# Decays of a blocked linear recurrence: from products with 0/1 matrices to one running sum and its differences

## What is computed

```python
b = jnp.cumsum(gc, axis=1)                       # running sum of the logs in a chunk
o_inter = jnp.einsum('bchk,bhkv->bchv', qc * jnp.exp(b), S)
diff = b[:, :, None] - b[:, None, :]
decay = jnp.exp(jnp.where(tril[None, :, :, None, None], diff, -jnp.inf))
scores = jnp.sum(qc[:, :, None] * kc[:, None] * decay, axis=-1)
o_intra = jnp.einsum('bijh,bjhv->bihv', scores, vc)
S = jnp.exp(b_last)[..., None] * S + jnp.einsum('bjhk,bjhv->bhkv', kc * jnp.exp(b_last[:, None] - b), vc)
```

## Time and profile before

| what | value |
|---|---|
| runs | 3353.06, 3353.88, 3355.38 us |
| median | 3353.88 us |
| profiled execution, first to last instruction | 3349.8 us |
| median less this span | 4.1 us |
| PE busy | 3183.6 us (95%) |
| DVE busy | 1477.6 us (44%) |
| ACT busy | 994.6 us (30%) |
| POOL busy | 638.9 us (19%) |
| mean granted TensorE clock | 0.984 |

### The profile page before, as it was taken

The page is one execution under the profiler, slowest core; times in us unless marked ns, Lnnn a source line. Parts: engine busy times, 40 slices in busy tenths (PEclk is TensorE's granted clock), DMA queues, the critical chain, the costliest instruction groups (busy, mean ns, idle before and its releaser), DMA issues. The chain is left out here.

```text
span 3349.8 us, 50802 instructions
## 1 busy us (share of the span) xinstructions
PE 3183.6 (95%) x19854; PEld 2885.0 (86%) x19854; DVE 1477.6 (44%) x2589; ACT 994.6 (30%) x2077; POOL 638.9 (19%) x951
## 2 busy tenths in 40 slices
PE   6999988988999999999989998898999999999999
PEld 5997666657999999999989966666589999999998
DVE  5312556655443344333372035665545443333443
ACT  4222345444321121211142233553433212111111
POOL 2113656521200000000031145663211000000000
PEclk8999999999999999999999999999999999999999
DMA  6415811103111111111123262111210111111101
GB/s 215 138 68 163 260 41 60 37 17 130 38 51 38 38 42 59 50 38 38 38 79 106 95 197 87 54 52 29 97 64 26 38 63 50 38 38 38 50 25 54
DMA packets 192340, 237.17 MB, mean 71 GB/s; under 512 B 18697, under 2 KB 166494, under 8 KB 192190
## 3 DMA queue, kind: packets, MB, share of 16 engines
q1 hardware_dynamic: 137276, 158.44, 14.7%
q10 hardware_dynamic: 44354, 45.25, 4.3%
q0 software_dynamic: 10560, 31.44, 2.6%
HBM read 195.53 MB, written 39.56 MB: 70 GB/s over the span
## 5 line engine op out<-in xcount | busy, mean ns | idle before, releaser
L1550 PE MATMUL banks<-act_split,w_split 128*128 128x384 f32 (+1 forms) x8352 | 1390.0, 327 | 11.1 <-DVE act_split L2294 11.1
L1550 PEld LDWEIGHTS banks<-act_split,w_split 128*128 128x128 f32 x8352 | 1378.4, 188 | 17.9 <-DVE act_split L2294 10.1
L1550 PE MATMUL banks<-hidden_split,w_split 128*128 128x384 f32 (+1 forms) x3168 | 528.3, 327 | 0.0
L1550 PEld LDWEIGHTS banks<-hidden_split,w_split 128*128 128x128 f32 x3168 | 524.7, 188 | 0.9 <-issue 0.6
L2352 DVE SCALAR_TENSOR_TENSOR x<-banks,mod,x 128x384 f32<-128x384 f32 (+2 forms) x768 | 353.6, 496 | 193.3 <-PE banks L1550 190.8
L2801 DVE TENSOR_TENSOR hidden_f<-banks,silu_a 128x384 f32<-128x384 f32 x132 | 70.7, 535 | 736.4 <-PE banks L1550 736.4
L1550 PE MATMUL banks<-w_split_tm,act_split 128*128 128x396 f32 (+1 forms) x1728 | 317.2, 344 | 0.0
L1550 PEld LDWEIGHTS banks<-w_split_tm,act_split 128*128 128x128 f32 (+1 forms) x1728 | 300.9, 182 | 13.2 <-issue 4.0
L1515 ACT ACTIVATE w_split<-w_raw 128x2048 fp32r<-128x2048 f32 x60 | 112.4, 1906 | 381.3 <-PE banks L1550 381.3
L1509 ACT ACTIVATE hidden_split<-hidden_f 128x384 fp32r<-128x384 f32 x132 | 67.0, 508 | 519.3 <-DVE hidden_f L2801 519.3
L620 POOL TENSOR_TENSOR norm_sum_n<-norm_sum_n,norm_sq 128x384 f32<-128x384 f32 (+1 forms) x42 | 43.3, 1032 | 798.8 <-ACT norm_sq L930 795.0
(11 more groups left out here) (235 smaller groups left out, 3254.7 us busy)
## 6 DMA issues: line engine op xcount, KB each, us to landing
w_raw<-in_w_ffn_in SPq DMA_DIRECT2D x44, 1024.0 KB, 5.1
w_mod_front<-in_w_mod ACTq DMA_DIRECT2D x76, 512.0 KB, 4.9
w_raw<-in_w_ffn_out SPq DMA_DIRECT2D x22, 1024.0 KB, 4.9
z_token_major<-z_stage POOLq DMA_DIRECT2D x64, 198.0 KB, 2.2
r_qkg<-z_feature_major SPq DMA_DIRECT2D x16, 576.0 KB, 4.3
r_v<-z_token_major SPq DMA_DIRECT2D x16, 512.0 KB, 3.7
w_raw<-in_w_o SPq DMA_DIRECT2D x8, 1024.0 KB, 7.1
w_mod_first<-in_w_mod SPq DMA_DIRECT2D x7, 1024.0 KB, 12.0
```

The lines of the kernel that those rows point to most:

```text
L1550: return T.matmul(out, lhsT, rhs, start=start, stop=stop, skip_group_check=True)
```

## The change

The logs are no longer turned and multiplied. DVE makes one running sum of a tile's logs along its 3 x 128 columns (`log_sums`, a scan that a 0/1 mask sets back every 64 columns) into `r_cum`, and the total of both chunks (`r_total`). For levels 2 to 32 it subtracts the sum at the border of the halves (`spans`: four subtractions of 192 columns for levels 2 and 4, six for 8, 16 and 32), and ACT takes the exponential in place (`near_decays`). For level 64 and the two sums of the whole tile, ACT adds the border's sum as a bias and takes the exponential at once (`far_decays`, five instructions in slot 4 and nine of 64 columns in slot 5). Level 1 needs no decay of the keys, so POOL copies them, and that of the queries is the log itself. In time: the scan of tile g + 1 stands on DVE in slot 6 behind `r_qi`, where the low half of the split was; its first subtractions in slot 7 behind the attention's copies, and its first exponentials on ACT in slot 7 where the first `decay` was; the six subtractions stand on DVE in slot 1 behind the recurrence's output, and their exponential on ACT in slot 2. For g0 the scan and the first subtractions stand ahead of the loop. Twice nine matmuls and three turns a tile leave PE, and the banks' plan (`R_BANK`) is made anew. The constant of the nine 0/1 matrices becomes the mask, a third as wide.

```diff
@@ -689,15 +685,18 @@
                 def decayed(g, lv):
                     r, b, i = (NLEV * g + lv) % 2, LEVELS[lv], lv // 3
                     if lv % 3 == 0:
-                        wait(pool, "r_act", l, f"e{g}_{i}2")
+                        wait(pool, "r_act", l, f"e{g}_{i}")
...
                     ee = rE[:, (3 * g + i) % 2, lv % 3]
                     blk = lambda x: x.rearrange("p f (n c) -> p f n c", c=2 * b)
-                    rstep(V.tensor_tensor(blk(rKB[:, r])[:, :, :, 0:b], blk(rZ[:, g % 2, 3:6])[:, :, :, 0:b],
-                                          blk(ee)[:, :, :, 0:b], ALU.mult), f"k{g}_{lv}")
+                    if lv == 0:
+                        rstep(V.tensor_copy(blk(rKB[:, r])[:, :, :, 0:b], blk(rZ[:, g % 2, 3:6])[:, :, :, 0:b]), f"k{g}_{lv}")
+                    else:
+                        rstep(V.tensor_tensor(blk(rKB[:, r])[:, :, :, 0:b], blk(rZ[:, g % 2, 3:6])[:, :, :, 0:b],
+                                              blk(ee)[:, :, :, 0:b], ALU.mult), f"k{g}_{lv}")
@@ -730,7 +729,7 @@
                     if h == 6:
-                        wait(pool, "r_pe", l, f"sd{g}")
+                        wait(pool, "r_act", l, f"e{g}_2")
                         rstep(V.tensor_tensor(rK2[:], rZ[:, u, 3:6], rE[:, (3 * g + 2) % 2, 2], ALU.mult), f"k2{g}")
                     elif h == 7:
                         vs = 0 if g < NTILE - 1 else 1
@@ -1048,58 +1047,61 @@
-                def g_hi(g):
...
-                def decay(g, i, f):
...
+                def near_decays(g, i):
+
+                    e = rE[:, (3 * g + i) % 2]
+                    if i == 0:
+                        if g:
                             wait(act, "r_pool", l, f"q{g - 1}_5")
                             wait(act, "r_dve", l, f"q{g - 1}_5")
+                        wait(act, "r_dve", l, f"c{g}")
+                        odd = lambda x: x.rearrange("p f (n c) -> p f n c", c=2)[:, :, :, 1]
+                        rstep(S.activation(odd(e[:, 0]), odd(rZ[:, g % 2, 6:9]), ACT.Exp), f"e{g}_01")
+                    wait(act, "r_dve", l, f"d{g}_{i}")
+                    x = e[:, 1 - min(i, 1):3]
+                    rstep(S.activation(x, x, ACT.Exp), f"e{g}_{i}")
+
+                def far_decays(g, half):
+
+                    e = rE[:, (3 * g + 2) % 2]
+                    lo, hi = rC[:, :, 0:64], rC[:, :, 64:P]
+                    if half == 0:
+                        wait(act, "r_pool", l, f"q{g}_2")
+                        wait(act, "r_dve", l, f"q{g}_2")
+                        rstep(S.activation(e[:, 0, :, 64:P], hi, ACT.Exp), f"e{g}_2r")
+                        rstep(S.activation(e[:, 1, :, 0:64], lo, ACT.Exp), f"e{g}_2b")
+                        for f in range(3):
+                            rstep(S.activation(e[:, 0, f, 0:64], lo[:, f], ACT.Exp, scale=-1.0, bias=rC[:, f, 63:64]), f"e{g}_2k{f}")
+                    else:
+                        wait(act, "r_dve", l, f"t{g}")
+                        for f in range(3):
+                            rstep(S.activation(e[:, 1, f, 64:P], hi[:, f], ACT.Exp, bias=rC[:, f, 63:64]), f"e{g}_2q{f}")
+                        for f in range(3):
+                            rstep(S.activation(e[:, 2, f, 0:64], lo[:, f], ACT.Exp, scale=-1.0, bias=rTL[:, f:f + 1]), f"e{g}_2l{f}")
+                        for f in range(3):
+                            rstep(S.activation(e[:, 2, f, 64:P], hi[:, f], ACT.Exp, scale=-1.0, bias=rC[:, f, P - 1:P]),
+                                  f"e{g}_2" if f == 2 else f"e{g}_2m{f}")
 
                 def r_slot(i):
                     g, h = divmod(i, 8)
                     if g < NTILE:
-                        if h == 0:
-                            decay(g, 0, 1)
-                            decay(g, 0, 2)
-                        elif h == 1:
-                            decay(g, 1, 0)
-                        elif h == 2:
-                            decay(g, 1, 1)
-                            decay(g, 1, 2)
+                        if h == 2:
+                            near_decays(g, 1)
...
                         elif h == 4:
-                            decay(g, 2, 0)
+                            far_decays(g, 0)
                         elif h == 5:
-                            decay(g, 2, 1)
-                            decay(g, 2, 2)
-                        elif h == 6 and g + 1 < NTILE:
-                            g_hi(g + 1)
+                            far_decays(g, 1)
                         elif h == 7:
...
                             if g + 1 < NTILE:
-                                decay(g + 1, 0, 0)
+                                near_decays(g + 1, 0)
...
                             z_square(0)
-                        elif j == 3 and p == 6:
-                            g_hi(0)
@@ -1266,7 +1266,7 @@
                 S.preload_act_table_set(table)
                 t8, n8 = ORDER[0], DEC_SEQ
                 load_mod(S, l, 1)
-                decay(0, 0, 0)
+                near_decays(0, 0)
                 for i in range(24):
                     if i == 0:
                         r_slot(0)
...
@@ -1791,35 +1769,16 @@
                 def r_slot(i):
                     g, h = divmod(i, 8)
                     if g < NTILE:
-                        if h == 0:
-                            sums(g, 0, 1)
-                            sums(g, 0, 2)
-                        else:
+                        if h:
                             levels(g, h - 1)
-                        if h == 1:
-                            sums(g, 1, 0)
-                        elif h == 2:
-                            sums(g, 1, 1)
-                            sums(g, 1, 2)
-                        elif h == 3:
+                        if h == 3:
                             diagonal(g)
-                        elif h == 4:
-                            sums(g, 2, 0)
-                        elif h == 5:
-                            sums(g, 2, 1)
-                            sums(g, 2, 2)
-                        elif h == 6 and g + 1 < NTILE:
-                            log_turn(g + 1)
                         elif h == 7:
                             key_turn(g)
-                            if g + 1 < NTILE:
-                                sums(g + 1, 0, 0)
...
-                pe.wait_ge(rm_ld, (l + 1) * 16)
-                sums(0, 0, 0)
@@ -2482,16 +2441,38 @@
                     if now:
                         own("a_dve", l, name)
 
-                def g_lo(g):
-                    wait(dve, "r_act", l, f"gh{g}")
-                    b = R_BANK["gT"]
-                    rstep(V.tensor_tensor(rGS[:, 1], ps[b][:, 0:384].rearrange("p (f t) -> p f t", f=3),
-                                          rGS[:, 0].bitcast(F32), ALU.subtract), f"gl{g}")
+                def log_sums(g):
+                    if g == 0:
+                        dve.wait_ge(rm_ld, (l + 1) * 16)
+                    else:
+                        wait(dve, "r_act", l, f"e{g - 1}_2")
+                    if g == NTILE - 1:
+                        wait(dve, "r_pool", l, "pad")
+                    dve.wait_ge(rz_ld[g % 2], (l * [5, 4][g % 2] + g // 2 + 1) * 16)
+                    rstep(V.tensor_tensor_scan(rC[:].rearrange("p f t -> p (f t)"), rM[:],
+                                               rZ[:, g % 2, 6:9].rearrange("p f t -> p (f t)"), 0.0, ALU.mult, ALU.add),
+                          f"c{g}", True)
+                    rstep(V.tensor_tensor(rTL[:], rC[:, :, 63], rC[:, :, P - 1], ALU.add), f"t{g}")
+
+                def spans(g, i):
+                    e = rE[:, (3 * g + i) % 2]
+                    if i == 0 and g:
+                        wait(dve, "r_pool", l, f"q{g - 1}_5")
+                    elif i == 1 and g:
+                        wait(dve, "r_pool", l, f"k2{g - 1}")
+                    for m in range(1 - i, 3):
+                        b = LEVELS[3 * i + m]
+                        blk = lambda x: x.rearrange("p f (n c) -> p (f n) c", c=2 * b)
+                        c, d = blk(rC[:]), blk(e[:, m])
+                        mid = c[:, :, b - 1:b].broadcast_to([P, 3 * P // (2 * b), b])
+                        rstep(V.tensor_tensor(d[:, :, 0:b], mid, c[:, :, 0:b], ALU.subtract), f"d{g}_{i}l{m}")
+                        rstep(V.tensor_tensor(d[:, :, b:2 * b], c[:, :, b:2 * b], mid, ALU.subtract),
+                              f"d{g}_{i}" if m == 2 else f"d{g}_{i}r{m}")
 
                 def decayed(g, lv):
                     m, b, i = NLEV * g + lv, LEVELS[lv], lv // 3
                     if lv % 3 == 0:
-                        wait(dve, "r_act", l, f"e{g}_{i}2")
+                        wait(dve, "r_act", l, f"e{g}_{i}")
@@ -2555,7 +2536,11 @@
                             wait(dve, "r_pe", l, f"o{g - 1}")
                         rstep(V.tensor_tensor(rQI[:], rZ[:, u, 0:3], rE[:, (3 * g + 2) % 2, 1], ALU.mult), f"qi{g}")
                         if g + 1 < NTILE:
```

(10 more changed lines are left out.)

## The result

The changed kernel takes 3411.12 us in the median (four runs, 3399.36 to 3415.29), the kernel before 3354.63 (3353.06 to 3356.41): ratio 1.0164, 95% interval 1.0151 to 1.0177. It is slower by some 56 us. The direction was forecast; the size was 10 us, and the range ended at 3386.

What follows compares the result with a forecast made beforehand. PE, busy 95%, was the only full engine, but was not taken to pace every stretch. Attention +7.7, fronts -3.9 and clock +6 gave +9.8 us on 3353.88, so 3364 us, range 3324 to 3386.

Steps and rivals of the forecast that it cites:

- The sum for g3: First wide attention tile: boundary wait holds the queries, +1.4 us, less 1.1 of savings, +0.3 a layer.
- the clock term: Attention tiles: longer PE gaps bring two more falls of the granted clock a layer, +6 us, between 0 and +14.
- The ceiling of 70 us: PE, 18 tiles of two layers: removed products save at most 70 us, reached only if PE paced every stretch.
- One sign of being right: Whole kernel: PE's busy time 60 to 75 us less, with the span not shorter.
- Tile boundaries: Slot 7 of narrow tiles: ACT's exponential waits for DVE's subtractions, delaying queries and scores, +6.1 us a layer with the scan.
- Narrow tiles, slots 0 to 6: g4 to g7: slot 0 wins 3.1 us a layer, late level 2 products cost 2.35, slots 4 to 6 win nothing.
- Fronts, -3.9: g0 to g2: part of PE's saved work comes through, -2.1 us in layer 0 and -1.8 in layer 1.
- Costs of the new instructions: DVE and ACT: subtraction 0.26 us alone, scan 0.72, 64-column exponential 0.2; ACT +0.8 us a tile.
- (a): Rival: PE paces after all and savings come through where it is over 90% busy: -30 us, 3324 us, chance 0.24.
- (b): Rival: boundary and slot 1 costs cancel front and slot 0 gains, no further clock fall: 3354 us, chance 0.20.
- (c): Rival: subtractions beside POOL take 0.45 us, slot 1 costs 2.7 us, deciding from 0.35 a subtraction: 3382 us, chance 0.14.

Runs made afterwards that it cites:

- the experiment on ACT's order: Changed kernel with the next tile's first exponentials behind the turned queries (and, at the front's end, the squares) on ACT: 3374.85 us, ratio 1.0065 to the kernel before.
- the first experiment: Kernel before with one matmul of each pair of 0/1 products left out and nothing added: 3353.27 us, ratio 0.999.
- the moved kernel: Changed kernel with all added work moved early into idle stretches, then mended in two places: 3359.37 us, ratio 1.0023 to the kernel before.
- the first filler experiments: Unused products put where PE waits, in the mended kernel with moved work (3353.27 us, 1.001) and in the kernel before (3343.06 us, 0.9967).

## Why the prediction was wrong, point by point

In short: two steps failed. The sum for g3 (+0.3 a layer) left out three waits, and the clock term (+6 in all) counted falls behind POOL's gaps only; the runs showed +14.5 and +11.4 us for g3, and 56.6 us more of lost clock.

*The ceiling of 70 us and that it isn't reached: right.* Leaving out 31.6 us of loads gave some 2 us. One sign of being right did not come: PE's busy time was to fall by 60 to 75 us and fell by 7.4, since the lower clock (0.966 in the mean instead of 0.984) stretched what was left: six products that took 1.04 us took 1.91 at 0.54.

*Tile boundaries: right in mechanism and nearly in size.* Forecast 1.65, 1.45, 1.2 and 1.0 us of lateness, with 0.2 each for the scan; the waits are 2.08, 1.86, 1.64 and 1.43 in both layers. The scan (0.94 us there and more, instead of 0.72) and the total behind it (0.39 us, not priced) could make the missing 0.2 us each; this was not taken apart. What the prediction didn't price is what follows such a wait: the experiment on ACT's order gave back 33 to 36 us, of which less than half is idle time.

*g3, +0.3 a layer: this step failed most, at +14.5 and +11.4.* The prediction treated the wide tile like a narrow one with one boundary. That boundary's wait came (2.73 us instead of 0.24, where +1.4 was forecast). It left out that a wide head has a second copy of the probabilities behind the recurrence's slot in DVE's order. The six subtractions of slot 1 delay that copy (a wait of 1.74 us where there was 0.80 one slot before). The scan of slot 6 does so again: the wait before the turned queries grew from 1.68 to 3.63, of which scan and total make 1.1 us and a product of DVE's just ahead, 1.23 us long instead of 0.50, another 0.7. And the squares behind the boundary's exponential make the first probabilities later (1.70 to 3.07 us, in layer 1 4.18 to 7.42). In layer 0 these waits stand in one tile with three stretches of low clock, 11 to 15 us each.

*Narrow tiles, slots 0 to 6: the gaps right, the sum too small.* The forecast said that the gap of g5 would grow from 1.90 to between 3 and 4 us, and that of g6 to over 2: 3.10 and 2.26. The product for level 2 was to come 0.9, 0.7 and 0.55 us late in g4, g5 and g6, and PE waits 1.10, 0.83 and 0.57 us for it. But the three tiles of layer 0 grew by 8.9 us, of which the boundaries are 5.6, where the 0.78 us won in each slot 0 were to make up for the lateness.

*Granted clock, +6: the term that was mis-sized.* The 1.7 us a fall rest on one stretch of 4 us at 0.57, behind the gap of 3.14 us in g4; behind the gap of 1.90 in g5 the clock was 1.00. That gaps of over 2 us would bring such falls was an estimate from these two. Four more were counted, all behind POOL's gaps in g5 and g6; three came (not the one of g5 in layer 0), with 1.7 us of lost clock each. Lost clock rose by 56.6 us, because the trace has falls behind the new waits in the wide tile, at boundaries and in the front too, where the prediction had priced the wait alone. So the 19 us of waits on the queries, with what hung on them, were worth 33 to 36 us.

*Fronts, -3.9: wrong in sign.* Layer 0's front took 5.8 us more, layer 1's about 1 (109 us before, 110 after, from the end of the input projection to the first scores); no DMA wait was won, and low stretches from 353 and 394 us, behind the rows that DVE made late in slot 1 of g1 and g2 (waits of 2.54 and 2.95 us), are new.

*Costs of the new instructions.* A subtraction is 0.35 us with starts 0.27 apart when alone (0.26 forecast), 0.40 on average. The narrow exponentials are 0.335, not 0.2; ACT's work grew by 1.5 us a tile, not 0.8 (the prediction's own terms for it add up to some 5.3 us, not 5.7). The scan, taken as 0.72, is 1.27 us on average, 0.94 at best (nine of the 18 took 0.94 to 0.95) and 1.78 at worst (at 416.14 us, with POOL at work); the average is below the 1.32 us set as the upper bound, the worst is above it.

*The rivals.* (a) fell with the first experiment, (b) with the result. (c) named the right sign and 3382 us, but its mechanism, subtractions slow beside POOL in slot 1, was at most a small part: at 0.40 us they are past its point of 0.35, yet moving them alone out of slot 1 gave 3 to 7 us, not clear of noise. The change also made a new plan of the banks; it was not varied by itself, and the moved kernel, which keeps it, is within 0.23% of the kernel before.

## What to carry to other kernels

Removing work from the fullest engine pays only where that engine sets the pace in the very stretch; a cheap test, halving the work and adding nothing, would have shown 0.1% before the replacement was written. New work on idle engines has to be placed by what stands behind it in that engine's order: 33 to 36 of some 56 us hung on two exponentials ahead of a copy and of the squares. And a new wait on TensorE can cost more than its length when the granted clock falls behind it: in this kernel 16.8 us less of idle time came with 22.2 us less of busy time.

## What the runs showed of the hardware

Unused products in PE's waits made the kernel before faster by 0.33%, with PE busier by 4 us. In the stretches about the filled waits the granted clock had been 0.52 to 0.57 of full speed for 41 us in the two layers; with filler it was 0.57 to 0.58 for 12. Equal gaps need not bring equal falls: behind 3.10 us of idle time the clock was 1.00 in one layer and 0.65 in the other. The built-in scan of 384 columns took 0.94 to 0.95 us nine times out of 18 and up to 1.78 else, a subtraction of the same width 0.545 on average. The 24 runs of the kernel before beside the first filler experiments spread over 16 us (3344.62 to 3360.72), so the span of a single trace is good to some 10 us; verdicts here rest on the ratios.
